# Recurrence factors: keys from the neighbouring column of the falling factor, two of four factors on GpSimd

## The reference, cut to what matters

```python
removed = jnp.einsum('zhvk,zhk->zhv', state, kh_t)
state = (state * w_t[:, :, None, :] - removed[..., None] * (kh_t * a_t)[:, :, None, :]
         + v_t[..., None] * k_t[:, :, None, :])
return state, jnp.einsum('zhvk,zhk->zhv', state, r_t)
```

## Time and profile before

| What | Value |
|---|---|
| median of 3 runs | 3562.02 us (3556.59 to 3572.75) |
| the profiled execution's own time | 3566.95 us |
| its span, from first to last instruction | 3565.2 us |
| PE busy | 3146.9 us, 88% |
| DVE busy | 2002.8 us, 56% |
| ACT busy | 1284.8 us, 36% |
| POOL busy | 910.2 us, 26% |

### The profile page before, as it was taken

How to read it: one execution, slowest core, us unless ns; L and a number is a source line. 1 busy time by engine, 2 the same in 40 slices (tenths; PEclk the granted TensorE clock), 3 DMA queues, 4 the chain that set the end, 5 groups by cost and what they waited for, 6 DMA issues and landing times. The chain is left out here.

```text
span 3565.2 us, 53470 instructions
## 1 busy us (share of the span) xinstructions
PE 3146.9 (88%) x21844; PEld 2464.7 (69%) x21844; DVE 2002.8 (56%) x2748; ACT 1284.8 (36%) x1613; POOL 910.2 (26%) x472
## 2 busy tenths in 40 slices
PE   7968999997999978999889998389997869999993
PEld 5446887796777756887678766268885358888882
DVE  3756551301433346553399447775644359998983
ACT  2543322222333333332232212312222247777772
POOL 3013443342222213443312300010100014454530
PEclk9989999999999989999999998699998979999996
DMA  3631222321111111222311100401001149999992
GB/s 137 235 119 71 94 94 83 124 95 71 60 60 60 60 48 71 94 94 84 106 48 60 59 17 1 176 23 50 26 26 75 47 168 360 364 372 367 374 355 100
DMA packets 76463, 439.37 MB, mean 123 GB/s; under 512 B 14832, under 2 KB 17904, under 8 KB 27376
## 3 DMA queue, kind: packets, MB, share of 16 engines
q1 hardware_dynamic: 66768, 427.12, 32.3%
q0 software_dynamic: 9504, 9.47, 0.8%
HBM read 421.85 MB, written 39.85 MB: 130 GB/s over the span
## 5 line engine op out<-in xcount | busy, mean ns | idle before, releaser
L76 POOL TENSOR_TENSOR ring_lo<-ring,unit_hi 128x2048 fp32r<-128x2048 f32 x116 | 536.2, 4624 | 1206.3 <-ACT unit_hi L71 1206.3
L122 PE MATMUL wide<-h_hi,unit_hi 128*128 128x512 f32 x1296 | 519.7, 401 | 99.9 <-DVE h_lo L182 43.5
L124 PE MATMUL wide<-h_hi,ring_lo 128*128 128x512 f32 x1296 | 519.1, 401 | 0.0
L123 PE MATMUL wide<-h_lo,unit_hi 128*128 128x512 f32 x1296 | 518.0, 400 | 0.0
L3013 DVE TENSOR_TENSOR ex_w_lo<-ring,ex_w_hi 128x2048 fp32r<-128x2048 f32 x192 | 437.2, 2287 | 43.5 <-ACT ex_w_hi L2966 41.6
L2966 ACT CAST ex_w_hi<-ring 128x2048 fp32r<-128x2048 f32 x192 | 365.7, 1908 | 103.7 <-DMA ring<-in_weights 91.1
L71 ACT CAST unit_hi<-ring 128x2048 fp32r<-128x2048 f32 x116 | 220.3, 1900 | 459.3 <-PE wide L124 450.7
L122 PEld LDWEIGHTS wide<-h_hi,unit_hi 128*128 128x128 f32 x1296 | 250.9, 194 | 178.6 <-POOL ring_lo L76 70.7
L123 PEld LDWEIGHTS wide<-h_lo,unit_hi 128*128 128x128 f32 x1296 | 247.0, 191 | 53.2 <-issue 0.2
L124 PEld LDWEIGHTS wide<-h_hi,ring_lo 128*128 128x128 f32 x1296 | 246.4, 190 | 52.7
L363 DVE TENSOR_TENSOR ffn_hidden_lo<-ffn_whole,ffn_hidden_hi 128x512 f32 (+1 forms) x44 | 201.5, 4579 | 50.6 <-ACT ffn_hidden_hi L338 50.6
(11 more groups left out here) (528 smaller groups left out, 6205.2 us busy)
## 6 DMA issues: line engine op xcount, KB each, us to landing
ring<-in_weights SPq DMA_DIRECT2D x356, 1024.0 KB
factors<-rp_out SPq DMA_DIRECT2D x8, 1536.0 KB, 5.5
rw_F<-factors SPq DMA_DIRECT2D x12, 1024.0 KB, 5.6
cb_both<-pair_rows_out SPq DMA_DIRECT2D x4, 1024.0 KB, 4.8
x<-in_x SPq DMA_DIRECT2D x1, 2048.0 KB, 7.5
x_kept<-x SPq DMA_DIRECT2D x1, 2048.0 KB, 12.2
x<-x_kept SPq DMA_DIRECT2D x1, 2048.0 KB, 8.9
x_mixing<-x SPq DMA_DIRECT2D x1, 2048.0 KB, 10.7
```

The costliest lines, as they stand in the source:

```text
L76: pool.tensor_tensor(self.lo[n % RING][:, :], self.ring[n % RING][:, :], self.hi[n % 2][:, :].bitcast(F32), ALU.subtract).then_inc(lo_read ...
L122: pe.matmul(dst, a[0], b[0], start=start, stop=False)
L123: pe.matmul(dst, a[0], b[1], start=False, stop=False)
L124: return pe.matmul(dst, a[1], b[0], start=False, stop=stop)
```

## The change

Keys (factor 0) need the falling product up to the token before. In the cumulative tile that is the same falling factor one column over. The new tile `down` therefore has 129 columns for each tile of 128 tokens: the 128 own columns and one more at the end where the product starts, filled by a small exponential of six columns from `edges`. VectorE reads `down` at `own` columns for factor 1 and at `other` columns (shifted by one) for factor 0. The exponential of the rate (L1827) and the product L1973 are gone. Factors 2 and 3 move from VectorE to a new GpSimd program; a new semaphore `grown_done` counts them, `exponents` waits for it before it overwrites buffers, and the store waits for both. GpSimd, like VectorE, waits for the store of step i-2 before it writes. VectorE's order within a step is now scan, factor 1, edge, factor 0, center. The tile `rp_reset0` moves by a few bytes.

```diff
-        e = nc.alloc_sbuf_tensor_at("rp_e", [P, RB, 2, TA], F32, offset=c.x_at)
+        up = nc.alloc_sbuf_tensor_at("rp_up", [P, RB, TA], F32, offset=c.x_at)
+        down = nc.alloc_sbuf_tensor_at("rp_down", [P, RB, TAT, P + 1], F32, offset=c.x_at + 4 * RB * TA)
...
+        own, other = (slice(1, P + 1), slice(0, P)), (slice(0, P), slice(1, P + 1))
...
                     sp.wait_ge(m_done, i + 1)
+                    sp.wait_ge(grown_done, i + 1)
...
                 def exponents(i):
+                    m, d = order[i]
                     act.wait_ge(s_ready, i + 1)
                     if i >= RB:
 
                         act.wait_ge(m_done, i - RB + 1)
-                    act.activation(sg[:, i, :], sg[:, i, :], ACT.Exp, scale=DECAY)
-                    act.activation(e[:, i % RB, 0, :], cum[:, i % RB, :], ACT.Exp, scale=-DECAY)
-                    act.activation(e[:, i % RB, 1, :], cum[:, i % RB, :], ACT.Exp, scale=DECAY).then_inc(exp_ready, 1)
+                        act.wait_ge(grown_done, i - RB + 1)
+                    act.activation(down[:, i % RB, :, own[d]], tiles(cum[:, i % RB, :]), ACT.Exp, scale=-DECAY)
+                    act.activation(down[:, i % RB, :, P * d:P * d + 1], edges[:, d, 0, m, :].unsqueeze(2), ACT.Exp, scale=DECAY)
+                    act.activation(up[:, i % RB, :], cum[:, i % RB, :], ACT.Exp, scale=DECAY).then_inc(exp_ready, 1)
...
                     dve.wait_ge(exp_ready, i + 1)
-                    dve.tensor_tensor(sg[:, i, :], sg[:, i, :], e[:, i % RB, 0, :], ALU.mult).then_inc(first_ready, 1)
                     if i + RB < N:
                         scan(i + RB)
...
-                    dve.tensor_tensor(x[:, :, 1, :], tiles(rr[:, m, :]), tiles(e[:, i % RB, 0, :]), ALU.mult)
+                    dve.tensor_tensor(x[:, :, 1, :], tiles(rr[:, m, :]), down[:, i % RB, :, own[d]], ALU.mult)
                     if i + RB < N:
                         edge(i + RB)
-                    dve.tensor_tensor(x[:, :, 2, :], tiles(r.a[:, m, :]), tiles(e[:, i % RB, 1, :]), ALU.mult)
+                    dve.tensor_tensor(x[:, :, 0, :], tiles(r.kh[:, m, :]), down[:, i % RB, :, other[d]], ALU.mult).then_inc(m_done, 1)
                     if i + RB < N:
                         center(i + RB)
-                    dve.tensor_tensor(x[:, :, 3, :], tiles(r.kmod[:, m, :]), tiles(e[:, i % RB, 1, :]), ALU.mult)
-                    dve.wait_ge(first_ready, i + 1)
-                    dve.tensor_tensor(x[:, :, 0, :], tiles(r.kh[:, m, :]), tiles(sg[:, i, :]), ALU.mult).then_inc(m_done, 1)
+
+            @block.gpsimd
+            def _(pool):
+                pool.wait_ge(minus_ready, MC)
+                pool.wait_ge(bonus_ready, MC)
+                for i, (m, d) in enumerate(order):
+                    x = out[:, i % RB, :, :, :]
+                    pool.wait_ge(exp_ready, i + 1)
+                    if i >= RB:
+
+                        pool.wait_ge(stored[i % RB], 16 * (i // RB))
+                    pool.tensor_tensor(x[:, :, 2, :], tiles(r.a[:, m, :]), tiles(up[:, i % RB, :]), ALU.mult)
+                    pool.tensor_tensor(x[:, :, 3, :], tiles(r.kmod[:, m, :]), tiles(up[:, i % RB, :]), ALU.mult).then_inc(grown_done, 1)
```

More of the change, by code:

```diff
@@ L1681, in rwkv_prepare_stage @@
         sg, cum = sb("sg", [P, N, TA]), sb("cum", [P, RB, TA])
-        rn, resets = sb("rn", [P, TA]), [nc.alloc_sbuf_tensor_at("rp_reset0", [P, TA], F32, offset=c.x_at + 4 * 2 * RB * TA), sb("reset1", [P, TA])]
-        e = nc.alloc_sbuf_tensor_at("rp_e", [P, RB, 2, TA], F32, offset=c.x_at)
+        rn, resets = sb("rn", [P, TA]), [nc.alloc_sbuf_tensor_at("rp_reset0", [P, TA], F32, offset=c.x_at + 4 * RB * (2 * TA + 8)), sb("reset1", [P, TA])]
+        up = nc.alloc_sbuf_tensor_at("rp_up", [P, RB, TA], F32, offset=c.x_at)
+        down = nc.alloc_sbuf_tensor_at("rp_down", [P, RB, TAT, P + 1], F32, offset=c.x_at + 4 * RB * TA)
         out = nc.alloc_sbuf_tensor_at("rp_out", [P, RB, TAT, 4, P], F32, offset=c.ring_at)
@@ L1696, in rwkv_prepare_stage @@
          spread, kh_ready, kmod_ready, rk_ready, minus_ready, bonus_done, bonus_ready, g_done, g_ready, turned, v_copied, reset_ready, scanned,
-         edges_ready, s_ready, exp_ready, first_ready, m_done, stored0, stored1, one_ka_ready, gain_step, edge_ready, gain_ready, padded) = c.semaphores("rp", (
+         edges_ready, s_ready, exp_ready, grown_done, m_done, stored0, stored1, one_ka_ready, gain_step, edge_ready, gain_ready, padded) = c.semaphores("rp", (
              "z_done", "sg_ready", "kap_ready", "sq_ready", "square_summed", "a_done", "a_ready", "grown_ready", "safe_ready", "root_ready",
              "rn_ready", "heads_ready", "spread", "kh_ready", "kmod_ready", "rk_ready", "minus_ready", "bonus_done", "bonus_ready", "g_done",
-             "g_ready", "turned", "v_copied", "reset_ready", "scanned", "edges_ready", "s_ready", "exp_ready", "first_ready", "m_done",
+             "g_ready", "turned", "v_copied", "reset_ready", "scanned", "edges_ready", "s_ready", "exp_ready", "grown_done", "m_done",
              "stored0", "stored1", "one_ka_ready", "gain_step", "edge_ready", "gain_ready", "padded"))
```

## The result

The changed kernel takes 3574.40 us (median of 12 runs, 3567.97 to 3581.18), the kernel before 3567.36 over as many (3556.59 to 3572.75). The ratio is 1.0022, with a 95% interval from 1.0012 to 1.0032: slower by 0.22%, some 8 us with 4 to 11 as ends. That is inside the half per cent that the forecast called no change, and inside its range of 3552 to 3580, and it lies on the side of the likeliest case. But the likeliest case had +4.0, so about half of the loss was not in the sum.

The account below looks back on a forecast made before the run. VectorE was taken to bound the 53.0 us loop, with the last store unhidden behind it. VectorE's 32.2 plus GpSimd's 24.8 make 57.0; 0.5 earlier start and 0.5 idle give +4.0, 3562.02 to 3566.0, range 3552 to 3580.

Parts of the forecast that it names:

- the likeliest case: Whole kernel: VectorE and GpSimd fully exclude each other in the loop; +4.0 us, median 3566.0, chance 0.72.
- VectorE's own work, 32.2: Eight-step loop: VectorE loses 24 instructions of 0.87 us, 20.9 in all, leaving 32.2 us of its own.
- Exclusion from rows 9 and 10: Loop: earlier ffn-stage overlaps show VectorE and GpSimd blocking each other; 16 GpSimd products at 1.55 us add 24.8.
- The scan counts: Each step's scan reads two SBUF tiles, so it was counted as excluded; otherwise the loop is about 7 us shorter.
- ACT's head start of 0.5: Loop start: with one exponential made six columns wide, the loop starts about 0.5 us earlier.
- "Neither engine waits" for stores: Loop: a store lands 5.6 us after its step, a step takes over 7, so VectorE and GpSimd never wait.
- steady step of 7.5: Profile of the loop: a step takes 4.41 + 3.1 = 7.5 us, against 7.01 before.
- The tail: After the loop: the last store's 5.97 us to the next stage's first DMA stays and shifts with the loop's end.
- The sum: Loop 32.2 + 24.8 = 57.0 us against 53.0, start 0.5 earlier, 0.5 idle time: +4.0.
- Side by side: Loop: VectorE and GpSimd run without blocking each other, 4.6 us a step; time 3544; chance 0.05.
- Dearer by rows: GpSimd's products pay 0.15 us for each row of 128, 12.0 in all; 3578; chance 0.06, rows or otherwise.
- the rival with gaps: Loop: GpSimd delays center, so VectorE waits for exponentials, 1 us a step, 6 in all; 3572; chance 0.07.

Follow-up runs that it names:

- the writes-only kernel: Changed kernel with GpSimd's two products a step replaced by three memsets that read nothing; loop 33.7 us, stretch to the next stage 42.9 us against 68.5.
- the three counts of instructions: Changed kernel (16 GpSimd products) against one factor back on VectorE (8) and a third GpSimd product a step (24); ratios to before 1.0022, 0.9998, 1.0049.

## Where the prediction was right and where it was wrong

- **VectorE's own work, 32.2.** Right: in the writes-only kernel VectorE takes 33.4 with one wait of 1.08 in it, and the step that met no GpSimd instruction took 4.41.
- **Exclusion from rows 9 and 10, in both directions.** Right. 1.55 for an instruction was 1.60 in the changed kernel, 25.6 in place of 24.8, and the three counts of instructions give the same.
- **The scan counts.** Right, as the 3.36 and GpSimd's 3.31 show. The edge copies, which I had left out of the exclusion, count too: 1.77 in place of 0.16. For the sum it is the same whether GpSimd's time falls on them or on the product behind them.
- **ACT's head start of 0.5.** It is 0.6: VectorE's first wait is 1.89 in place of 2.50.
- **"Neither engine waits" for stores.** Wrong as a statement, harmless for the sum: GpSimd waits for stores 17.5 us in all, since its step starts as early as its buffer allows, but it is not GpSimd's idle time that counts. For the same reason no steady step of 7.5 was seen; the mean is 7.9.
- **The tail.** This is the step that failed. The prediction took the last store's 5.97 as fixed and moved it with the loop's end. It had noted that steps 6 and 7 have two VectorE instructions each, with four of GpSimd's left, and put idle time of 0.5 for it. What it did not ask is when the last store but one is issued, nor what GpSimd does to the gain, which is drawn out from 2.2 to 6.9 and pushes VectorE's last four factors together. The two stores now meet, the last lands in 8.3 in place of 5.5, and the tail has 2.8 more.
- **The sum.** 57.0 + 0.5 for idle time against 57.8, and 5.97 against 8.81: +4.0 forecast, +7.0 in the trace. The loop was right for the reason given, to 0.3 us. That the total still came out inside the range owes something to the range, which was made wide for the scatter of the medians. The 18 us that the forecast took as the least that can be told from no change were too coarse: with 12 runs each the interval is about 4 us to either side, and no change lies outside it.
- **The rivals.** Side by side is ruled out by all kernels in which GpSimd reads. Dearer by rows is ruled out too: an instruction that stood behind nothing took 1.80 with its six rows, as the line through rows 8 had it (1.82). Of the waits at the exponentials that the rival with gaps had, there are none on VectorE behind the first; ACT waits, for VectorE's center.

## What to carry to other kernels

In this kernel, work that went from VectorE to GpSimd gave nothing where VectorE's instructions beside it read two SBUF tiles: a product of 768 columns cost 0.87 on VectorE and 1.60 there, and it cost this although GpSimd was idle and the step had room. What GpSimd did for nothing was memsets, which only write. Before moving work, look in the trace for a place where the two engines already overlap, as rows 9 and 10 did. When a loop ends in a store, follow the last two stores, not only the last: the distance between them decided here how long the last one took.

## What the runs showed of the hardware that was not expected

- GpSimd's writes alone leave VectorE's two-input instructions at full speed (24 memsets of 0.74 added nothing to VectorE's 32.2 and one wait for a store), and one SBUF input is enough to stop them (0.59 for a copy of 0.82).
- Copies of six columns on VectorE show longer records beside memsets (0.97 in place of 0.16), where the two-input products do not, and what follows the copies is not late. Beside GpSimd's products they show 1.77, and there VectorE does stand.
- A 1.5 MB store issued 1.7 us behind another took 8.3 to land, 2.6 behind 7.4, 3.5 behind two others 6.8, and 5.5 in the median, with the DMA engines at 380 GB/s in the first case.
